# Expert weights asked for in column quarters, routing ahead of a low part, and a first token tile scaled by ScalarE in a two-layer hybrid kernel

## The chip, the cores and the metric

The kernel runs on one core of one Trainium2 chip. The metric is device microseconds from start to end of one execution. The core has TensorE (PE in the profile, with its weight loads as PEld), VectorE (DVE), ScalarE (ACT), GpSimd (POOL) and SyncE (SP), whose queue issues all DMAs of this kernel. Engines run on their own and meet at semaphores.

## What is computed

Two layers over 512 tokens of width 1024, in float32. Cut to what matters here:

```python
for l in range(2):
    h = rms_norm(x, norm_mix_g[l])
    parts = split(h @ w_in[l])            # attention, spatial gate, state space, branch gates
    y_a, y_b, y_c = attention(parts), spatial_gating(parts), s5_layer(parts)
    x = x + (g_a * y_a + g_b * y_b + g_c * y_c) @ w_mix_o[l]
    h = rms_norm(x, norm_ffn_g[l])
    # router: best of 4 groups, then the 2 best of its 8 experts, for every token
    x = x + sum over the 2 chosen experts e of weight * ((silu(h @ w_gate[e]) * (h @ w_up[e])) @ w_down[e])
out = rms_norm(x, norm_final_g)
```

There are 32 experts. The gate, up and down weights of each are 2 MB, so a layer streams 192 MB of expert weights.

## The kernel before

Tokens lie in 4 tiles of 128 (NT = 4), the width in 8 parts of 128 (ND = 8). Many products are made from a rounded high part and a low remainder (h_hi and h_lo, w_hi and w_lo, x_hi and x_lo), to keep float32 precision. Each engine has a hand-written order of work; nothing is scheduled by a planner.

**Prologue (L411 to L474).** ScalarE squares the four token tiles (`square_tokens`, L356), VectorE scales each tile (L366) and TensorE transposes it into two PSUM banks (`turn_tile`, L381). VectorE also prepares rope angles; ScalarE takes their two sines (L471, L473) at the end. All engines meet at the end of the block, and the layer's block starts.

**Start of a layer.** SyncE asks for the small tables (L520 to L523). VectorE multiplies the transposed tiles by the norm's weights, two operations of 128x512 for each tile, into `hT` (L1463). TensorE waits for the first tile (`hT_ready`) and starts `token_job` (L671). VectorE waits for `step_ready` from ScalarE (L1218, which waits for small tables), runs a long chain of small operations for the state space layer, then makes `h_lo` of the four tiles (`low_tokens`, L1532) between low parts of weights (L1545). The first `feature_job` (L649) needs `h_hi` and low weights, and for its last 8 products (x16 and x8 in the trace are one job's records) the `h_lo` of all four tiles.

**End of the dense part.** TensorE mixes (L968), transposes tiles for the router (L988), computes logits (L1000), ranks tokens within experts (L1008, L1015) and gathers the tokens of the first four experts (`gather_tile`, L1026). VectorE's order for tile 3 is `take_h2(3)`, `inverse(3)`, `low_part(3, 0, 4)` (L1843), `route(3)` (L1851 to L1867), `placed(3)` (L1874, L1875), `low_part(3, 4, 8)`, then `take` (L1922) of the gathered tokens twice, once for each half of the width. `low_part` needs `x_hi` of the tile from ScalarE (L1382); `route` needs the logits from TensorE.

**Experts.** They go in 16 pairs. For a pair, TensorE does gate and up of expert 0 and of expert 1 (`gate_up`, L1109, L1110, 6.9 us each), adds back the rows of the pair before (L1083, L1084), gathers for the next quad (L1072, L1074), transposes, and multiplies by the down weights of both (L1100). In the last two pairs nothing is gathered. Weights have two places, one for each expert of a pair. SyncE's loop asks for gate and up of expert 2i+2+b when `gu_done` reaches 2i+b+1 (L511, L512), and for both down weights of the next pair when `down_done` reaches 2i+2 (L515). The 12 MB of the first pair are asked for before the loop.

**Between the layers.** The last rows are added, squared, scaled and transposed into PSUM for the next layer. Every engine reads the largest token count of an expert and branches on it (none overflows). `clear` (L2308) is a barrier (L2312), a clearing of about 190 semaphores by SyncE, and a second barrier (L2314). The next layer's block follows.

Of the kernel before, what the change touches and what calls it, by code (L numbers as in the profile page):

```python
# [22 lines left out]
ALU = mybir.AluOpType  # L23
# [3 lines left out]
P = 128  # L27
D = 1024
S = 512
L = 2  # L30
NT = S // P
# [79 lines left out]
QUAD = 4 * CAP  # L111


def build(nc, io):
    ctx = ExitStack()
    with ctx:
# [46 lines left out]
        hT = view(O_HT, ND, S)  # L163
        slab = [O_SLAB + i * SLAB for i in range(3)]
# [213 lines left out]
        def turn_tile(t):  # L378

            for d in range(ND):  # L380
                nc.tensor.transpose(ps[:, BANK_X[t][d // 4], (d % 4) * P:(d % 4 + 1) * P], x_unit[:, t, d * P:(d + 1) * P], ident)  # L381

        def turn_tokens(pe, g):

            for t in range(NT):
                pe.wait_ge(g["xn"], t + 1)
                turn_tile(t)
# [12 lines left out]
        stack_made = so["ov_y"]  # L400

# [9 lines left out]
        with nc.Block() as block:  # L411
# [14 lines left out]
            def _(pe):  # L426
                pe.wait_ge(s["pro_in"], 32)
                turn_tokens(pe, turn_g)
# [36 lines left out]
            def _(act):  # L465
# [30 lines left out]
        shared = dict(nsa_parted="ov_silu", outp_free="ov_weights", m_hi_ready="ov_sel", m_lo_ready="ov_gathered", br_hi_ready="ov_xe", br_lo_ready="ov_gu",  # L496
# [4 lines left out]
        for layer in range(L):  # L501
# [15 lines left out]
            with nc.Block() as block:  # L517
                @block.sync
                def _(sp):
# [72 lines left out]
                    with sp.Fori(0, N_EXP // 2 - 1) as i:  # L592
# [24 lines left out]
                def _(pe):  # L617
# [34 lines left out]
                    def nsa_job(t):  # L652

                        for k in range(ND):
                            r = 32 * (k % 4)
                            last = nc.tensor.matmul(ps[r:r + 32, BANK_S[0], t * P:(t + 1) * P], wnsa[k], hT[:, k, t * P:(t + 1) * P],
# [10 lines left out]
                    def token_job(n, w, lo, hi, t):  # L667

                        out = bank_p(n)
                        for k in range(ND):  # L670
                            last = nc.tensor.matmul(out[:, 0:hi - lo], hT[:, k, t * P:(t + 1) * P], w[:, k, lo:hi],  # L671
# [14 lines left out]
                    for t in range(NT):  # L686
                        pe.wait_ge(s["hT_ready"], t + 1)
# [425 lines left out]
                    def pair(i, m, at, first, second, last_quad):  # L1113

                        q = at % 2
                        for b in range(2):
                            pe.wait_ge(w_in_sem[b][0], 16 * i + 16)
                            pe.wait_ge(w_in_sem[b][1], 16 * i + 16)
                            if b == 1 and not first:
                                pe.wait_ge(s["y_read"], 2 * i - 1)  # L1120
# [1307 lines left out]
```

## Time and profile before

| | |
|---|---|
| time, median of 3 runs | 1911.43 us (1910.63 to 1912.46) |
| the profiled execution | 1910.96 us, span 1909.2 us |
| TensorE busy | 1848.6 us, 97% |
| VectorE, ScalarE, GpSimd busy | 52%, 25%, 8% |
| HBM read | 476.59 MB, 252 GB/s over the span |

An engine's busy share alone doesn't say what bounds a stretch. The timeline says what runs when and how long an engine was idle before it; the waits name who ended the idle time; the windows give DMA rate and granted clock for a stretch; the DMA view tells how long each transfer took from issue to landing.

### The profile page before, as it was taken

How to read it: one execution, taken by the hardware profiler on the slowest of the kernel's cores; microseconds unless marked ns; L12 is line 12 of the kernel's file. 1: busy time of each engine (PE TensorE's matmuls, PEld its weight loads, DVE VectorE, ACT ScalarE, POOL GpSimd, SP SyncE). 2: the span in 40 equal slices, each digit the busy share in tenths (PEclk: the TensorE clock that was granted, in tenths of full speed). 3: DMA queues.
4: the chain of work that ended last, by engine and by line, in shares of the span. 5: the costliest groups of instructions: out<-in, count | busy, mean ns of one | idle time of the engine just before them, and what ended most of it. 6: DMA issues, size and time to landing. Idle time of an engine off the chain costs nothing. (4 is left out here: it accounts for less than half of the span.)

```text
span 1909.2 us, 26714 instructions
## 1 busy us (share of the span) xinstructions
PE 1848.6 (97%) x10376; PEld 1156.9 (61%) x10377; DVE 990.3 (52%) x1929; ACT 483.7 (25%) x858; POOL 151.2 (8%) x241
## 2 busy tenths in 40 slices
PE   6999999999999999999889999999999999999996
PEld 3777777778545445454347877778775445455442
DVE  7755556667334343343478555567673344343344
ACT  4413444432111111111234234444321110111112
POOL 4600000050000000000054000000500000000000
PEclk9999999999999999999989999999999999999998
DMA  4222111344999999999722221114359999999994
GB/s 170 67 98 85 67 67 45 111 140 190 377 428 427 419 428 427 427 428 417 314 65 77 95 68 65 67 45 133 118 226 423 427 424 425 429 427 427 423 428 175
DMA packets 59952, 482.13 MB, mean 253 GB/s; under 512 B 9808, under 2 KB 22608, under 8 KB 30672
## 3 DMA queue, kind: packets, MB, share of 16 engines
q1 hardware_dynamic: 59856, 480.80, 62.1%
q8 instruction: 66, 1.08, 0.2%
q14 instruction: 30, 0.25, 0.0%
HBM read 476.59 MB, written 4.19 MB: 252 GB/s over the span
## 5 line engine op out<-in xcount | busy, mean ns | idle before, releaser
L1932 DVE TENSOR_TENSOR x_tokens<-x_tokens,ps 128x512 f32<-128x512 f32 x240 | 160.3, 686 | 216.5 <-PE ps L1084 215.5
L1109 PE MATMUL ps<-slabs,arena 128*64 128x512 f32 x512 | 228.4, 599 | 4.3 <-issue 4.3
L1110 PE MATMUL ps<-slabs,arena 128*64 128x512 f32 x512 | 228.4, 600 | 0.0
L1100 PE MATMUL ps<-arena,branch 128*64 128x512 f32 x512 | 227.0, 596 | 0.5 <-ACT branch L1403 0.5
L1100 PE MATMUL ps<-slabs,branch 128*64 128x512 f32 x512 | 227.0, 595 | 0.0
L1109 PE MATMUL ps<-arena 128*64 128x512 f32 x512 | 225.0, 592 | 0.9 <-DVE arena L1922 0.9
L1110 PE MATMUL ps<-arena 128*64 128x512 f32 x512 | 225.0, 592 | 0.0
L822 PE MATMUL ps<-h_hi,w_parts 128*128 128x512 f32 x768 | 210.8, 408 | 1.5 <-DVE w_parts L1545 1.5
L1109 PEld LDWEIGHTS ps<-slabs,arena 128*64 128x64 f32 x512 | 70.7, 138 | 151.9 <-issue 151.9
L822 PEld LDWEIGHTS ps<-h_hi,w_parts 128*128 128x128 f32 x768 | 135.1, 189 | 38.8 <-issue 9.2
L1109 PEld LDWEIGHTS ps<-arena 128*64 128x64 f32 x512 | 70.0, 137 | 145.8 <-issue 145.8
L1100 PEld LDWEIGHTS ps<-arena,branch 128*64 128x64 f32 x512 | 67.3, 137 | 133.7 <-issue 132.7
L1938 DVE TENSOR_TENSOR branch<-ps,branch 64x512 f32<-64x512 f32 x64 | 44.1, 689 | 196.2 <-ACT branch L1399 195.3
L1399 ACT ACTIVATE branch<-ps 64x512 f32<-64x512 f32 x64 | 37.9, 592 | 399.6 <-PE ps L1110 399.6
L1977 DVE SCALAR_TENSOR_TENSOR split_rows<-ps,arena,split_rows 128x512 fp32r<-128x512 f32 x64 | 48.0, 751 | 147.1 <-ACT split_rows L1409 147.1
L1409 ACT ACTIVATE split_rows<-ps,arena 128x512 fp32r<-128x512 f32 x64 | 44.0, 687 | 308.3 <-PE ps L1100 291.7
L1545 DVE TENSOR_TENSOR w_parts<-slabs,w_parts 128x512 fp32r<-128x512 f32 x176 | 119.3, 738 | 4.5 <-ACT w_parts L1228 3.9
L1072 PE MATMUL ps<-split_rows,h_lo 128*128 128x256 f32 x448 | 115.4, 281 | 0.0
L1074 PE MATMUL ps<-split_rows,x_lo 128*128 128x256 f32 x448 | 115.1, 280 | 0.0
L822 PE MATMUL ps<-h_lo,w_parts 128*128 128x512 f32 x384 | 108.1, 406 | 0.0
L1083 PE MATMUL ps<-split_rows 128*128 128x512 f32 x240 | 103.9, 433 | 0.0
L1228 ACT ACTIVATE w_parts<-slabs 128x2048 fp32r<-128x2048 f32 x50 | 95.5, 1909 | 30.9 <-DMA slabs<-in_dense 30.9
(361 smaller groups left out, 3094.0 us busy)
## 6 DMA issues: line engine op xcount, KB each, us to landing
arena<-in_expert_w_gate SPq DMA_DIRECT2D x32, 2048.0 KB, 12.1
slabs<-in_expert_w_gate SPq DMA_DIRECT2D x32, 2048.0 KB, 15.0
slabs<-in_expert_w_up SPq DMA_DIRECT2D x32, 2048.0 KB, 19.4
arena<-in_expert_w_up SPq DMA_DIRECT2D x32, 2048.0 KB, 16.5
arena<-in_expert_w_down SPq DMA_DIRECT2D x32, 2048.0 KB, 9.5
slabs<-in_expert_w_down SPq DMA_DIRECT2D x32, 2048.0 KB, 13.9
slabs<-in_gate_w SPq DMA_DIRECT2D x24, 1024.0 KB, 4.8
slabs<-in_dense SPq DMA_DIRECT2D x22, 1024.0 KB, 5.8
```

Source lines behind the costliest of these rows:

```text
L822: last = nc.tensor.matmul(fill.out, wp[:, k % ND, (n % 2) * P:(n % 2 + 1) * P], hp[:, k % ND, :], start=(k == 0), stop=(k == GATE_MM - 1))
L1072: nc.tensor.matmul(ps[:, bank + part // 4, col:col + QUAD], x_hi[:, t, d * P:(d + 1) * P], sel[:, t, :], start=(t == 0), stop=False)
L1074: last = nc.tensor.matmul(ps[:, bank + part // 4, col:col + QUAD], x_lo[:, t, d * P:(d + 1) * P], sel[:, t, :], start=False, stop=(t == NT ...
L1083: nc.tensor.matmul(out, to, y_hi[:, cols], start=True, stop=False)
L1100: done = nc.tensor.matmul(ps[64 * b:64 * b + 64, BANK_Y[half], :], hidT[:, k, CAP * b:CAP * (b + 1)], w_down[b][:, k, half * 512:(half + 1 ...
L1109: nc.tensor.matmul(ps[0:64, BANK_GU[b], :], xk, low[:, k, :], start=(k == 0), stop=(k == ND - 1), tile_position=(0, 0))
L1110: return nc.tensor.matmul(ps[64:P, BANK_GU[b], :], xk, high[:, k, :], start=(k == 0), stop=(k == ND - 1), tile_position=(0, 64))
L1228: nc.scalar.activation(w_hi[k % 3], view(slab[k % 3], SLAB // 2), ACT.Identity).then_inc(s["w_hi_ready"], 1)
L1545: v.tensor_tensor(w_lo[k][:, part], view(slab[k], SLAB // 2)[:, part], w_hi[k][:, part], ALU.subtract)\
L1932: v.tensor_tensor(xs, xs, ps[:, banks[n % len(banks)], :], ALU.add).then_inc(s["back_added"], 1)
L1938: v.tensor_tensor(hid[rows], ps[other, BANK_GU[b], :], silu[rows], ALU.mult).then_inc(s["hid_done"], 1)
L1977: v.scalar_tensor_tensor(y_lo[:, cols], ps[:, BANK_Y[half], :], w_slot, y_hi[:, cols], ALU.mult, ALU.subtract).then_inc(s["y_lo_ready"], 1)
```

## The change

1. **Quarters (GU_PARTS = 4).** For expert 2, the third, gate and up are each asked for in four column quarters of 512 KB, after `gate_up` of expert 0 has done 2, 4, 6 and 8 of its 8 parts. The first pass of SyncE's loop is written out, and the loop starts at 1. TensorE's waits for the first weight place count the 3 more landings.
2. **Routing order.** For tile 3, `route(3)` stands ahead of `low_part(3, 0, 4)`.
3. **First gathered tokens.** Of the 4 parts in each half, VectorE takes 2 (one operation of half the size) and ScalarE the other 2, each 128x256 from PSUM with a scale (`xe_first`).
4. **First token tile.** ScalarE scales the 8 parts of tile 0 at the end of the prologue, and of layer 0 for layer 1, into a place of its own (`hT_first`, where `xsT` and `h2T` are at other times). VectorE does tiles 1 to 3 in the layer's block. TensorE's first `token_job` waits for nothing from that block but the weights. The two sines of the prologue move into ScalarE's part of layer 0.
5. **Waits and clearing.** TensorE's waits for `y_read`, each beside one for `y_lo_ready`, are gone. Between the layers the barrier ahead of the clearing is gone.

```diff
+GU_PARTS = 4
+        hT_first = view(O_XS, ND, P)
+        def tile_of(t):
+            return hT_first if t == 0 else hT[:, :, t * P:(t + 1) * P]
+        def first_tile(layer, told):
+            for d in range(ND):
+                nc.scalar.activation(hT_first[:, d, :], ps[:, BANK_X[0][d // 4], (d % 4) * P:(d % 4 + 1) * P], ACT.Identity,
+                                     scale=gmix[:, 8 * layer + d:8 * layer + d + 1]).then_inc(told, 1)
...
                 square_tokens(act, turn_g, pro_x)
-                act.wait_ge(s["pro_dve"], N_REDUCE)
-                nc.scalar.activation(rope_sin, rr, ACT.Sin).then_inc(s["pro_act"], 1)
-                act.wait_ge(s["pro_dve"], 2 + N_REDUCE)
-                nc.scalar.activation(rope_cos, r2, ACT.Sin).then_inc(s["pro_act"], 1)
-                act.wait_ge(s["pro_act"], 2)
+                act.wait_ge(s["pro_gmix"], 16 * L)
+                act.wait_ge(first_turned, 1)
+                first_tile(0, first_turned)
...
-                    with sp.Fori(0, N_EXP // 2 - 1) as i:
+                    for part in range(GU_PARTS):
+                        if part < GU_PARTS - 1:
+                            sp.wait_ge(s["gu_part"], part + 1)
+                        else:
+                            sp.wait_ge(s["gu_done"], 1)
+                        cols = slice(part * SLAB // GU_PARTS, (part + 1) * SLAB // GU_PARTS)
+                        for m, name in enumerate(("expert_w_gate", "expert_w_up")):
+                            sp.dma_start(w_place[0][m][:, cols], expert_rows(io[name], 2, ND)[:, cols]).then_inc(w_in_sem[0][m], 16)
+                    sp.wait_ge(s["gu_done"], 2)
+                    load_gate_up(sp, 3, 1)
+                    sp.wait_ge(s["down_done"], 2)
+                    for b in range(2):
+                        load_down(sp, 2 + b, b)
+                    with sp.Fori(1, N_EXP // 2 - 1) as i:
...
-                        pe.wait_ge(s["hT_ready"], t + 1)
+                        if t >= 1:
+                            pe.wait_ge(s["hT_ready"], t)
...
-                        pe.wait_ge(s["y_read"], 2 * i)
                         pe.wait_ge(s["y_lo_ready"], 2 * i)
...
+                                if first and b == 0 and k % 4 >= 2:
+                                    pe.wait_ge(s["xe_first"], 2 * (k // 4) + k % 4 - 1)
                                 done = gate_up(k, b, i, m, at)
+                                if first and b == 0 and k < ND - 1 and (k + 1) % (ND // GU_PARTS) == 0:
+                                    done.then_inc(s["gu_part"], 1)
...
+                    for half in range(2):
+                        act.wait_ge(s["x_gathered"], half + 1)
+                        for k in (4 * half + 2, 4 * half + 3):
+                            nc.scalar.activation(xe[0][:, k, :], ps[:, BANK_GATHER0 + 2 * half + 1, (k % 2) * QUAD:(k % 2 + 1) * QUAD], ACT.Identity,
+                                                 scale=small["gffn"][:, k:k + 1]).then_inc(s["xe_first"], 1)
...
+                    if not last_layer:
+                        act.wait_ge(s["next_turned"], 1)
+                        first_tile(layer + 1, s["next_turned"])
...
-                    for t in range(NT):
+                    for t in range(1, NT):
...
                     inverse(3)
+                    route(3)
                     low_part(3, 0, 4)
-                    route(3)
                     placed(3)
                     low_part(3, 4, ND)
...
-                        take(0, half, BANK_GATHER0 + 2 * half)
+                        v.tensor_tensor(xe[0][:, 4 * half:4 * half + 2, :], ps[:, BANK_GATHER0 + 2 * half, :].rearrange("p (b c) -> p b c", c=QUAD),
+                                        gf(4 * half, 2, QUAD), ALU.mult).then_inc(s["xe_ready"], 1)
...
-                clear(nc, layer_sems)
+                nc.sync.sem_clear(range(layer_sems[0].num, layer_sems[-1].num + 1))
+                nc.all_engine_barrier()
```

## Rows read from the trace of the kernel before

**Rows 1.** TensorE's waits, whole span: line, who ended them, sum, times, longest.
```profile
PE ps L1008 <- DVE arena L1867: 5.1, 4, 1.7
PE ps L1109 <- issue: 4.3, 2, 2.3
```

**Rows 2.** Timeline, prologue's end: start, duration, engine, line, then idle before.
```profile
16.13 0.20 ACT L351 ACTIVATE arena<-arena 128x1 f32<-128x1 f32 x1 [1.08 <-DVE arena L372]
...
18.41 0.63 ACT L473 ACTIVATE arena<-xn_tokens 128x512 f32<-128x512 f32 x1
...
19.52 4.87 DVE L1463 TENSOR_TENSOR hT<-ps,arena 128x512 f32<-128x512 f32 x8 [1.15 <-PEq L411]
...
20.96 13.97 PE L671 MATMUL ps<-slabs,hT 128*128 128x512 f32 x32 [2.49 <-DVE hT L1463]
```

**Rows 3.** ScalarE's durations: two of the timeline, and a page group (mean ns).
```profile
51.29 0.60 ACT L1239 ACTIVATE arena<-ps 128x512 f32<-128x512 f32 x1
51.78 0.41 ACT L1242 ACTIVATE branch<-arena 128x256 f32<-128x256 f32 x1
...
L1409 ACT ACTIVATE split_rows<-ps,arena 128x512 fp32r<-128x512 f32 x64 | 44.0, 687 | 308.3 <-PE ps L1100 291.7
```

**Rows 4.** Timeline, layer 0: the last h_lo and the products that need it.
```profile
53.55 1.22 DVE L1532 TENSOR_TENSOR h_lo<-hT,h_hi 128x1024 fp32r<-128x1024 f32 x1
...
54.91 2.02 PE L649 MATMUL ps<-h_lo,w_parts 128*128 128x512 f32 x8
```

**Rows 5.** Timeline: start of layer 1, and its last h_lo.
```profile
964.62 4.87 DVE L1463 TENSOR_TENSOR hT<-ps,arena 128x512 f32<-128x512 f32 x8 [8.51 <-PEq L2314]
...
999.28 1.23 DVE L1532 TENSOR_TENSOR h_lo<-hT,h_hi 128x1024 fp32r<-128x1024 f32 x1 [0.31 <-PE ps L656]
...
1002.81 1.98 PE L649 MATMUL ps<-h_lo,w_parts 128*128 128x512 f32 x8
```

**Rows 6.** SyncE's wait at the second barrier between the layers.
```profile
SPq L2314 <- PEq L2314: 0.5, 1, 0.5
```

**Rows 7.** Timeline, layer 0: TensorE and VectorE from tile 3's logits to expert 0.
```profile
466.01 1.87 PE L1000 MATMUL ps<-arena,branch 128*128 128x36 f32 x16
...
468.59 1.24 DVE L1843 SCALAR_TENSOR_TENSOR x_lo<-x_tokens,arena,h_lo 128x512 fp32r<-128x512 f32 x1 [2.33 <-ACT h_lo L1382]
469.74 0.25 DVE L1851 SCALAR_TENSOR_TENSOR arena<-ps,arena 128x36 f32<-128x36 f32 x1
...
473.43 0.41 PE L1008 MATMUL ps<-arena 128*128 128x32 f32 x2 [1.71 <-DVE arena L1867]
...
474.90 0.74 PE L1026 MATMUL ps<-split_rows,h_lo 128*128 128x256 f32 x4 [0.40 <-DVE split_rows L1875]
...
477.52 0.61 PE L1109 MATMUL ps<-arena 128*64 128x512 f32 x1 [0.47 <-DVE arena L1922]
```

**Rows 8.** Window 480 to 484: busy times, clock, DMA share, GB/s; expert 2's gate issue.
```profile
480.00:484.00 4.00, 4.00 (x21) 1.58 (x19) 3.73 (x9) 0.62 (x2) 0.00 (x0) 1.00 0.19 78
...
484.80 0.35 SPq L511 DMA_DIRECT2D arena<-in_expert_w_gate  x1
```

**Rows 9.** DMA view of 484 to 496, last figure us to landing: expert 2's gate.
```profile
arena<-in_expert_w_gate SPq DMA_DIRECT2D x1, 2048.0 KB, 7.8
```

**Rows 10.** DMA view, first down weight of a pair, issued at 503.4, 829.0, 888.2.
```profile
arena<-in_expert_w_down SPq DMA_DIRECT2D x1, 2048.0 KB, 9.6
...
arena<-in_expert_w_down SPq DMA_DIRECT2D x1, 2048.0 KB, 8.6
...
arena<-in_expert_w_down SPq DMA_DIRECT2D x1, 2048.0 KB, 10.1
```

**Rows 11.** Timeline, layer 0, expert 31's gate and up: the first, and a slow one.
```profile
922.82 0.61 PE L1109 MATMUL ps<-slabs,arena 128*64 128x512 f32 x1 [1.98 <-issue]
...
924.33 1.06 PE L1109 MATMUL ps<-slabs,arena 128*64 128x512 f32 x1
```

**Rows 12.** Window 6 to 8 us, loads of x and weights: last three clock, DMA share, GB/s.
```profile
6.00:8.00 2.00, 0.00 (x0) 0.00 (x0) 1.22 (x3) 0.20 (x1) 1.08 (x4) 1.00 1.03 413
```

More of the change, by code:

```diff
@@ L380, in turn_tile, with turn_tokens @@
             for d in range(ND):
-                nc.tensor.transpose(ps[:, BANK_X[t][d // 4], (d % 4) * P:(d % 4 + 1) * P], x_unit[:, t, d * P:(d + 1) * P], ident)
-        def turn_tokens(pe, g):
+                last = nc.tensor.transpose(ps[:, BANK_X[t][d // 4], (d % 4) * P:(d % 4 + 1) * P], x_unit[:, t, d * P:(d + 1) * P], ident)
+            return last
+        def first_tile(layer, told):
+            for d in range(ND):
+                nc.scalar.activation(hT_first[:, d, :], ps[:, BANK_X[0][d // 4], (d % 4) * P:(d % 4 + 1) * P], ACT.Identity,
+                                     scale=gmix[:, 8 * layer + d:8 * layer + d + 1]).then_inc(told, 1)
+        def turn_tokens(pe, g, told):
             for t in range(NT):
                 pe.wait_ge(g["xn"], t + 1)
-                turn_tile(t)
+                last = turn_tile(t)
+                if t == 0:
+                    last.then_inc(told, 1)
         s = {n: sem(n) for n in ("pro_in", "pro_gmix", "pro_table", "pro_dve", "pro_act", "pro_x0", "pro_x1", "pro_x2", "pro_x3")}
@@ L670, in token_job @@
                         for k in range(ND):
-                            last = nc.tensor.matmul(out[:, 0:hi - lo], hT[:, k, t * P:(t + 1) * P], w[:, k, lo:hi],
+                            last = nc.tensor.matmul(out[:, 0:hi - lo], tile_of(t)[:, k, :], w[:, k, lo:hi],
                                                     start=(k == 0), stop=(k == ND - 1))
@@ L1116, in pair @@
                         for b in range(2):
-                            pe.wait_ge(w_in_sem[b][0], 16 * i + 16)
-                            pe.wait_ge(w_in_sem[b][1], 16 * i + 16)
+                            more = 0 if first or b == 1 else 16 * (GU_PARTS - 1)
+                            pe.wait_ge(w_in_sem[b][0], 16 * i + 16 + more)
+                            pe.wait_ge(w_in_sem[b][1], 16 * i + 16 + more)
                             if b == 1 and not first:
-                                pe.wait_ge(s["y_read"], 2 * i - 1)
                                 pe.wait_ge(s["y_lo_ready"], 2 * i - 1)
@@ L1174, in _ @@
                     for half in range(2):
-                        pe.wait_ge(s["y_read"], N_EXP - 1 + half)
                         pe.wait_ge(s["y_lo_ready"], N_EXP - 1 + half)
@@ L1185, in _ @@
                             pe.wait_ge(s["next_xn"], t + 1)
-                            turn_tile(t)
+                            last = turn_tile(t)
+                            if t == 0:
+                                last.then_inc(s["next_turned"], 1)
                 @block.scalar
@@ L1223, in _ @@
                     nc.scalar.activation(cos1, sincos[3], ACT.Sin).then_inc(s["polar_ready"], 1)
+                    if layer == 0:
+                        nc.scalar.activation(rope_sin, rr, ACT.Sin).then_inc(s["pro_act"], 1)
+                        nc.scalar.activation(rope_cos, r2, ACT.Sin).then_inc(s["pro_act"], 1)
                     def split_hi(k):
@@ L1531, in low_tokens @@
                         cols = slice(t * P, (t + 1) * P)
[L1532 removed]
+                        v.tensor_tensor(h_lo[:, :, cols], tile_of(t), h_hi[:, :, cols], ALU.subtract).then_inc(s["h_lo_ready"], 1)
                     lows = [0]
@@ L1632, in rope @@
                         dve.wait_ge(s["rot_done"], i + 1)
+                        if layer == 0 and i == 0:
+                            dve.wait_ge(s["pro_act"], 2)
                         part = ps[:, BANK_T[i % 2], :]
@@ L2224, in _ @@
                         square_tokens(act, turn_g, None)
+                        if not last_layer:
+                            act.wait_ge(first_turned, 1)
+                            first_tile(layer + 1, first_turned)
                     @block.sync
```

15 lines of the change are left out of this document (8 added, 7 removed).

## The prediction, made before the changed kernel was seen

> **What bounds the kernel now.** I read the page first: TensorE is busy for 1848.6 of 1909.2 us, so a change can win little more than TensorE's idle time, and each piece of it has to be read where it lies. The waits say who ends it [rows 1]. Three places matter here: the start of each layer, the stretch from the router to the first expert, and the last expert of each layer. The timeline gives each its size. In layer 0 TensorE waits 2.49 us for its first product [rows 2], 1.71, 0.40 and 0.47 us on the way to expert 0 [rows 7], and 1.98 us for expert 31's weights [rows 11]; layer 1 repeats these (2 of 2 in [rows 1] for expert 31, 2.3 us there), with a longer start.
>
> The expert stretch has two limits that nearly meet. A middle pair takes TensorE 29.6 us, and the 12 MB of a pair take the DMA engines about 29.5 us. The proof is the landing time of a pair's first down weight: 9.6 us after its issue in the first pair, 8.6 in the twelfth, so DMA gains about 0.1 us a pair; then it loses 1.5 us within two pairs (10.1) [rows 10]. The last pairs are shorter for TensorE (25.8 us, nothing is gathered), and DMA, with that backlog, is 2 us late for expert 31.
>
> **Prologue and start of layer 0.** ScalarE drops two sines at the end of the prologue and gets 8 scalings of 128x128 from PSUM. No row has that shape. From 0.60 us for 512 columns and 0.41 for 256, 128 columns take about 0.31; the scale from memory adds 0.09 (0.687 against 0.60); two in a row overlap by 0.11 (the second begins 0.49 after the first) [rows 3]. So 8 x 0.29 + 0.1 = 2.4 us, from 16.33, where its last root ends, to 18.75; before, the sines ended at 19.04 [rows 2]. Bounds: with no per-column part 8 x 0.2 = 1.6, with 0.41 each and no overlap 3.3. The block then starts 0.3 us earlier (between 0.7, VectorE's own end, and -0.6). TensorE needs no VectorE operation any more: its first product moves from 20.96 to about 19.35, 0.15 us after the block's start at 19.2, 1.6 us earlier. The first weights landed by 17.1, ahead of it.
>
> Most of this is lost 35 us later. `feature_job` needs `h_lo` of tile 3, ready at 54.77, and uses it at 54.91: slack 0.1 us [rows 4]. VectorE's chain to it has no idle time above chain latency from 24.5 on, and it begins with ScalarE's `step_ready`, which waits for small tables asked for at the block's start. Taking 2 of 8 operations off VectorE ahead of that (1.2 us) therefore gives nothing; the chain moves by the block's 0.3 us only. The two sines, 1.3 us on ScalarE ahead of its first evacuation, delay that to about 30.4, and TensorE wants the bank at 34: hidden by 3 us. Gain in layer 0: 0.3 + 0.1 slack, **0.35 us** (0 to 0.8).
>
> A rule speaks against moving this: the Trainium skill ("ScalarE: Activation LUTs", Rules for kernel authors) sends plain multiplies to VectorE. The trace agrees that VectorE is quicker here, 2 x 0.6 against 2.4 us [rows 2, 3]; by the rule the move would cost 1.2 us a layer. I don't follow it, because the work falls where ScalarE has nothing else.
>
> **Between the layers.** ScalarE's 2.4 us fall into the 8.5 us in which VectorE and ScalarE stand still, while TensorE transposes the other tiles: hidden. TensorE's start behind the block's start shrinks from 1.44 us (964.62 to 966.06) to about 0.15: 1.3 us. One barrier less: the remaining one was waited for 0.5 us [rows 6]; with the clearing that now runs beside TensorE's branch I take 0.7 (0.4 to 1.2). Here nothing takes it back: the last `h_lo` is ready at 1000.51, after a wait for TensorE itself, and used at 1002.81, slack 2.3 us [rows 5]. **2.0 us** (1.5 to 2.6).
>
> **Router to expert 0, each layer.** The logits of tile 3 are out at 467.9, yet `route(3)` starts at 469.74, behind `x_hi` and `low_part` [rows 7]. Moved ahead, it starts 1.8 us earlier and ends at 471.6, where TensorE has just run out of gathers (471.7): `rank(3)` at 471.75 instead of 473.43. Now `low_part` (1.24 us) lies between `route` and `placed`, till 472.8, while the rank is there at 472.5: 0.25 us are given back, so the gather of tile 3 goes from 474.90 to 473.45, 1.45 us. Its second low half is there in time (by 474.5, used at 475.0). The first gathered half then costs VectorE one operation of half the size (0.69 us) instead of 1.24, beside TensorE's last gathers, and the 0.47 us wait goes. ScalarE's parts take 0.5 us each and are wanted 1.7 us after the first. Expert 0 starts at 475.6, not 477.52: **1.9 us** a layer (1.4 to 1.95). Its gate and up landed by 473.
>
> **Quarters, each layer.** DMA runs dry at about 481 (share 0.19 in 480 to 484) and expert 2 is asked for at 484.8 [rows 8], landing 7.8 us later [rows 9]. The first quarter's request comes at about 477.4, while the queue is still full, so the stream goes on without a gap and expert 2's weights land 5.3 us earlier. But the next request, expert 2's down weight, waits for `down_done`, which moves only with TensorE, 1.9 us. It landed 9.6 us after its issue, and a transfer into an empty queue takes 7.8 to 8.2. So the lead is cut: DMA can gain 9.6 - 8.0 = 1.6 us on TensorE, of which 0.6 to 1.0 was gained by itself later anyway (8.6) [rows 10]. After the 1.5 us that DMA loses, the landing is at 9.4 instead of 10.1: **0.7 us** (0.6 to 0.9) off the wait for expert 31. It stays, with 1.3 us in layer 0 and 1.6 in layer 1.
>
> The clock is the larger part. After the wait of 1.98 us six pairs of products ran slow, at 1.06 instead of 0.59 us, a granted 1.2 GHz; they were 1.7 us longer [rows 11]. Layer 1's wait of 2.31 was followed by the same, 1.7 us. The waits of 1.71 us ahead of `rank(3)` were not: expert 0's products run at 0.61 [rows 7]. With 1.3 and 1.6 us both new waits are below that, so I take **1.7 us** a layer (0 to 1.7).
>
> TensorE's dropped waits for `y_read` stood beside waits that imply them: 0, at most 0.05 a pair.
>
> **Sum.** 0.35 + 2.0 + 2 x (1.9 + 0.7 + 1.7) = 10.95, about 11 us. The profiled execution took 1910.96, which makes 1900.0; it was 0.5 below the median, so 1900.5 for the median.
>
> **Rivals.**
> 1. *The clock still falls* after the shorter wait, in one layer or both: 1.7 or 3.4 us less gain, 1902.2 to 1903.9. For it: only two rows tell where the line lies, and 1.6 is near 1.71.
> 2. *The wait for expert 31 goes wholly*, if DMA keeps more of its 5.3 us lead or loses less near the end: 1.3 + 1.6 us more, 1897.6. Against: the 7.8 to 8.2 us floor is seen in all first requests.
> 3. *The saved microseconds are handed on*: `placed` or ScalarE's parts come last instead and the clearing is on the path. Half of 2.0 and of 2 x 1.9 gone, and the clock too: 1904 to 1908. It covers the case that an edit doesn't do what it says.
> 4. *Slower: the quarters are slow transfers.* If eight transfers of 512 KB needed more than the 9.8 us of two whole ones by over 5.3 us, expert 2 would land later than before and, since DMA makes up only 0.1 us a pair, the whole stream would end later. The gain of 0.35 + 2.0 offsets 1.2 a layer, so the kernel is slower from 6.5 us extra a layer. At twice the time, 9.8 us extra, it would be 2 x 4.5 - 2.35, about 1918. Against: x is loaded in pieces of 512 KB with the same rows of 4 KB, beside weights, at 413 GB/s [rows 12]. The Trainium skill ("DMA: Bandwidth & Descriptors", Measured and Anatomy of one DMA) advises at least 1 MiB a transfer and gives 2.0 us fixed for each; six more transfers in a row would by that be an estimated 12 us extra a layer, and the result about 1922. The trace disagrees, since transfers in flight overlap.
>
> **How the numbers follow.** Forecast 0.5, rival 1 0.22, rival 2 0.13, rival 3 0.11, rival 4 0.04. The bounds of the terms widen each by 1 us or so; the range from 1896.5 to 1905 holds the forecast, rivals 1 and 2 and part of rival 3, leaving out some 0.15. A difference under 0.2% (3.8 us) can't be told from none. Faster 0.91: all but rival 4 and the worse half of rival 3. Same 0.06, slower 0.03.
>
> **What would show it.** The changed trace should have TensorE's first product near 19.35 and a new wait of about 1.2 us for `h_lo` in layer 0; in layer 1 no such wait; no wait of 1.7 at `rank(3)`; DMA share 1.0 without a gap around 482, and a short gap near 502 instead; a wait of 1.3 to 1.6 us ahead of expert 31, with its products at 0.59 after it. Products at 1.06 there speak for rival 1, no wait at all for rival 2, a later landing of expert 2 than 20 us after expert 0's start for rival 4. The step most likely wrong is the floor of 8 us and what follows for the clock.

## The result, and the profile after

The changed kernel takes 1895.64 us (median of 4 runs, 1893.32 to 1896.33), against 1911.16 for the kernel before beside it: a ratio of 0.9916, 95% interval 0.9903 to 0.9929, so 13.6 to 18.5 us faster. The forecast of 1900.5 was 4.9 us too high and its range began at 1896.5. A second set of runs gave 1896.19 and a ratio of 0.9931 (0.9917 to 0.9946).

The page of the changed kernel, profiled in a run of 1896.33 us (before: 1910.96 us, span 1909.2, TensorE busy 1848.6):

```profile
span 1894.6 us, 26685 instructions
PE 1843.7 (97%) x10376; PEld 1153.4 (61%) x10377; DVE 983.2 (52%) x1925; ACT 489.2 (26%) x881; POOL 151.4 (8%) x241
PEclk9999999999999999999989999999999999999998
```

Its waits of TensorE over the whole span (line, who ended them, sum, times, longest), which answer to [rows 1]:

```profile
PE ps L386 <- DVE arena L371: 16.6, 4, 11.8
PE ps L1135 <- issue: 4.2, 2, 2.7
PE ps L995 <- ACT w_parts L1262: 2.5, 1, 2.5
PE ps L697 <- PEq L2300: 1.9, 1, 1.9
PE ps L1035 <- DVE arena L1912: 1.7, 2, 0.9
...
PE ps L675 <- DVE h_lo L1575: 1.3, 1, 1.3
...
PE ps L1126 <- DMA slabs<-in_expert_w_down: 1.2, 1, 1.2
...
PE ps L697 <- issue: 0.9, 1, 0.9
```

The 1.7 us waits for the rank of tile 3 are gone (L1035 now has two of 0.9, for tile 2's rank), the predicted new wait for `h_lo` is there with 1.3 us, and expert 31 still waits twice (L1135). The stretches between the same instructions of both profiles put the 14.6 us of span as follows (us, after less before):

| stretch | change |
|---|---|
| start to the router's tables, layer 0 | -0.1 |
| from there to the request of expert 1's gate | -1.2 |
| that request to expert 0, layer 0 | -2.0 |
| expert 0 to the end of the turns | -0.9 |
| end of the turns to the next layer's block | -3.9 |
| block to VectorE's last `h_lo` of layer 1 | +0.9 |
| from there to the request of expert 1's gate | -1.2 |
| that request to expert 0, layer 1 | -2.0 |
| expert 0 to the request of the last norm's weights | -2.5 |
| from there to the last output's request | +0.9 |
| that request to the end | -2.6 |

The routing (-2.0 twice) is as forecast. Some entries are the clock's: in layer 0 slow products followed TensorE's wait of 2.43 us in the mix stage of the kernel before, and none followed the 2.53 us there in the changed one (-1.2); the same holds for expert 31 in both layers (-0.9 with a wait that is 0.7 longer, and -2.5 with one that is 0.8 shorter). In layer 1 the +0.9 and the -1.2 behind it belong together: TensorE reaches the products that need this `h_lo` 38.2 us after the block's start before and 37.9 after.

Two entries are neither forecast nor the clock's: the gap between the layers (3.9 us for a barrier costed at 0.7) and the very end (2.6 us, in which the change touches nothing). Both have one cause. Each instruction of a line has a row in the view of that line, also those of an engine's sequencer that the page leaves out. The columns are line, queue, kind, count, duration in ns (min/median/max) and start. These are the jumps of TensorE's sequencer past code that is not run (the rare path for overfull experts), in the kernel before, between the layers and at the end:

```profile
L2312 PEldq COMPARE_BRANCH  x1: 3677/3677/3677, 959.7 to 959.7; - x1
L2254 PEldq COMPARE_BRANCH  x1: 3446/3446/3446, 1905.4 to 1905.4; - x1
```

And in the changed kernel:

```profile
L2299 PEldq COMPARE_BRANCH  x1: 348/348/348, 955.4 to 955.4; - x1
L2304 PEldq COMPARE_BRANCH  x1: 348/348/348, 1893.4 to 1893.4; - x1
```

The other engines take 0.05 to 0.07 us for theirs and then stand at the barrier. SyncE's waits in the kernel before have a row for it:

```profile
SPq L2312 <- PEq L2312: 3.6, 1, 3.6
```

The DMA view of 959.5 to 964.6 in the kernel before, and of 955 to 961 in the changed one, shows pieces of 16 KB on a queue that carries instructions, two and one:

```profile
q8 instruction: 2, 0.03, 2.9%
```
```profile
q8 instruction: 1, 0.02, 1.6%
```

In all profiles here such a piece of 16 KB starts 0.9 to 1.1 us into each long jump and another behind it; with a short jump the first starts 1.1 us or more after the jump's start, when the jump is over. That the long jump waits for its piece fits this, but no run shows it by itself, and a piece takes only 0.9 to 1.6 us.

### The profile page after: what moved, and what is told of

It reads as the page before. It is cut to its first block and busy times, and to the rows that moved or that the text cites. A ratio compares the mean times of both kernels' runs of the same rounds, so it can differ in the third digit from the quotient of the medians.

```text
span 1894.6 us, 26685 instructions
## 1 busy us (share of the span) xinstructions
PE 1843.7 (97%) x10376; PEld 1153.4 (61%) x10377; DVE 983.2 (52%) x1925; ACT 489.2 (26%) x881; POOL 151.4 (8%) x241
## 3 DMA queue, kind: packets, MB, share of 16 engines
q8 instruction: 65, 1.06, 0.2%
## 5 line engine op out<-in xcount | busy, mean ns | idle before, releaser
L1135 PE MATMUL ps<-slabs,arena 128*64 128x512 f32 x512 | 225.0, 592 | 4.2 <-issue 4.2
L1135 PE MATMUL ps<-arena 128*64 128x512 f32 x512 | 225.1, 592 | 0.4 <-DMA arena<-in_expert_w_up 0.4
L1136 PE MATMUL ps<-slabs,arena 128*64 128x512 f32 x512 | 225.0, 592 | 0.0
L1135 PEld LDWEIGHTS ps<-slabs,arena 128*64 128x64 f32 x512 | 70.0, 137 | 150.2 <-issue 150.2
L849 PEld LDWEIGHTS ps<-h_hi,w_parts 128*128 128x128 f32 x768 | 135.0, 188 | 38.8 <-issue 9.2
L1135 PEld LDWEIGHTS ps<-arena 128*64 128x64 f32 x512 | 69.9, 137 | 145.7 <-issue 145.4
L1262 ACT ACTIVATE w_parts<-slabs 128x2048 fp32r<-128x2048 f32 x50 | 95.5, 1910 | 30.9 <-DMA slabs<-in_dense 30.9
## 6 DMA issues: line engine op xcount, KB each, us to landing
slabs<-in_expert_w_gate SPq DMA_DIRECT2D x32, 2048.0 KB, 14.9
```

Source lines behind the costliest of these rows:

```text
L849: last = nc.tensor.matmul(fill.out, wp[:, k % ND, (n % 2) * P:(n % 2 + 1) * P], hp[:, k % ND, :], start=(k == 0), stop=(k == GATE_MM - 1))
L1135: nc.tensor.matmul(ps[0:64, BANK_GU[b], :], xk, low[:, k, :], start=(k == 0), stop=(k == ND - 1), tile_position=(0, 0))
L1136: return nc.tensor.matmul(ps[64:P, BANK_GU[b], :], xk, high[:, k, :], start=(k == 0), stop=(k == ND - 1), tile_position=(0, 64))
L1262: nc.scalar.activation(w_hi[k % 3], view(slab[k % 3], SLAB // 2), ACT.Identity).then_inc(s["w_hi_ready"], 1)
```

## The experiments

Each kernel was profiled once and timed beside the kernel before on the same chip. Differences in us are the ratio's, taken of 1910 us.

**after_again.** The changed kernel, no edit.

> The changed kernel itself, once more. Theory A (the stream of expert weights ends the mixture stage): in both layers the first product of expert 31 waits 1.5 us, the first product on the last down weights waits about 1.2 us, and the 2.7 us wait and the late landing of 18.6 us that the first profile shows ahead of expert 31 of layer 0 are one slow stretch of transfers in that execution and do not come again. Rival (the forecast's rule, that waits of up to 1.7 us leave the clock alone and waits of 2.0 us and more don't): a fall of the clock after every wait of 2.0 us or more, and none after shorter ones. Theory B for the 2.5 us by which the span ends sooner after the last output is issued (5.6 us before, 3.0 us after): if it belongs to the program it comes again; if it is one execution's, the new profile can have either. Time 1893 to 1896.5 in each case.

1896.19 us. The wait ahead of expert 31 is 1.0 and 0.9 us, and no clock falls behind it; but it falls behind the 2.0 us wait in the mix stage of layer 0, where the first profile had waited 2.5 us without a fall. The landing of 18.6 us (the up weight of the last pair of layer 0, ahead of the 2.66 us wait) did not come again, so it is not the program's; 18.1 to 18.4 us, with waits of 2.66 to 2.68, come in three other kernels here (tile_dve, low_first, y_waits_back). The short end came again (3.0 us after the last output's request). That the stream of weights ends the stage is not borne out: the last down weights were not waited for here.

**barrier_only and barrier_back.** One barrier dropped from the kernel before, and put back into the changed one.

```
-                clear(nc, layer_sems)
+                nc.sync.sem_clear(range(layer_sems[0].num, layer_sems[-1].num + 1))
+                nc.all_engine_barrier()
```

> The kernel before with one part of the change alone: between the layers the semaphores are cleared by one clear and one barrier in place of barrier, clear, barrier. Theory A (read off the two traces: from the end of the turns to the start of the next layer's block 5.8 us before, 1.9 us after): 3.9 us faster than before, 1907.3. Rival (the term of the forecast): 0.7 us faster, 0.4 to 1.2, so 1910.5. Rival 2: the gap shrinks by 3.9 us in the trace, but the layer's first products then wait for VectorE's first tile, which has to be scaled first, and half of it is lost again: 1909.

> The changed kernel with the first of the two barriers between the layers put back. Theory A: 3.9 us slower than the changed kernel, about 1899.5, and the gap between the turns' end and the next block is 5.8 us again. Rival (the forecast's term): 0.7 us slower, about 1896.4. Under A nearly all of the difference between the forecast of 10.95 us and the measured 15.5 us is this one term.

barrier_only: 1910.23, ratio 1.0003 (0.9992 to 1.0014), no difference. The gap falls from 5.8 to 4.6 us, and the jump in it still takes 3.4. barrier_back: 1898.01, 0.9939 (0.9922 to 0.9956), 1.8 us over after_again at the median, with intervals that overlap; its gap is 2.4 us against 1.9. So the barrier is worth 0.6 to 1.1 us of the gap, as the forecast had it, and the reading "3.9 us for the barrier" is wrong. In the total it can't be told.

**whole_loads and quarters_only.** The quarters taken out of the changed kernel, and put alone into the kernel before.

```
-                    for part in range(GU_PARTS):
-                        ...
-                    with sp.Fori(1, N_EXP // 2 - 1) as i:
+                    with sp.Fori(0, N_EXP // 2 - 1) as i:
```

> The changed kernel with the third expert's gate and up weights asked for whole after its place's last product, as before; all else as changed. Theory A (the stream of expert weights ends the stage, so each layer pays what its stream starts later, 0.8 us, whatever the clock does at expert 31, since a slower product there only shortens the wait for the last down weights): 0.8 us per layer, 1.6 us slower than the changed kernel in all, about 1897.2, with waits ahead of expert 31 of 2.3 us in both layers. Rival 1 (the forecast's terms: 0.7 us of wait and 1.7 us of clock per layer): 4.8 us slower, about 1900.5. Rival 2: the transfers have slack and nothing is lost, 1895.6.

> The kernel before with the quarters alone. Theory E (a lead of the transfers is lost again within three pairs: in the changed kernel the landing time of a pair's up weight starts at 15.2 us in the second pair against 17.0 before, and is 16.4 to 17.0 by the fifth, from where it goes on as with whole loads): no difference to before, 0 +- 1 us, wait ahead of expert 31 between 1 and 2.5 us. Rival (the forecast): 0.7 us a layer off the wait and the clock behind it saved, 1.7 us a layer: 4.8 us faster.

whole_loads: 1895.01, 0.9929 (0.9913 to 0.9945), the same as after_again beside it; its waits ahead of expert 31 are 1.48 and 1.53 us, not 2.3, and no slow products follow them. quarters_only: 1908.60, 0.9994 (0.9984 to 1.0004): 1.1 us faster, -0.8 to 3.1, which leaves out the 4.8 us of the first forecast. The quarters are worth nothing that can be told here. The DMA view says where the lead goes. It shows the time from issue to landing (last figure) of the up weight of the second pair, in the kernel before, where it is issued at 510.9:

```profile
arena<-in_expert_w_up SPq DMA_DIRECT2D x1, 2048.0 KB, 16.8
```

In the changed kernel, issued at 507.7:

```profile
arena<-in_expert_w_up SPq DMA_DIRECT2D x1, 2048.0 KB, 15.2
```

The lead is there, 1.6 us in layer 0 (0.8 in layer 1, 16.1 against 16.9). The pairs after it read 15.9, 17.0, 16.8 against 16.7, 16.4, 16.8: two pairs on it is gone. It went the same way in layer 1 (16.1, 16.2, 16.7, 17.2, 18.3) and in quarters_only (14.9, 15.6, 15.9, 17.1). In all profiles this time falls by 0.1 to 0.3 us a pair over most pairs and rises again, by 0.4 to 2.6 us over one or two pairs, at places that differ; so whoever starts ahead need not end ahead. What makes the rises was not tried.

The signs against slow quarters came too: the eight pieces moved at 402 to 412 GB/s (476 to 488 us), expert 2's last piece landed 17.8 us after expert 0's start (before: 20.2), the DMA share at 480 to 484 is 1.02 instead of 0.19, and 0.80 at 500 to 504.

**no_y_waits and y_waits_back.** TensorE's waits on `y_read`, which stand beside waits that imply them, out of the kernel before and back into the changed one.

```
                         pe.wait_ge(s["selT_read"], i)
-                        pe.wait_ge(s["y_read"], 2 * i)
                         pe.wait_ge(s["y_lo_ready"], 2 * i)
...
-                                pe.wait_ge(s["y_read"], 2 * i - 1)
...
-                        pe.wait_ge(s["y_read"], N_EXP - 1 + half)
```

> The kernel before with one part of the change alone: TensorE's waits on y_read are taken out (the waits on y_lo_ready that stand beside them are kept); nothing moves but the length of TensorE's program. Theory C (where TensorE's instructions lie in its program decides it): in the kernel before two jumps of TensorE's sequencer take 3.7 and 3.5 us, with a fetch of 16 KB of instructions beside each, one between the layers and one at the very end, and every engine stands at a barrier behind them; in the changed kernel the same jumps take 0.35 us, and its program has these waits fewer. So both become short here, the stretch from the turns' end to the next layer's block falls from 5.8 to about 2.5 us and that from the last output's issue to the end from 5.6 to 3.0: 5.9 us faster than before. Rival 1 (the forecast's step: these waits cost nothing): no difference. Rival 2: the program's length matters, but by another number of instructions than these: the jumps stay long here.

> The changed kernel with TensorE's waits on y_read put back, all else as changed. Theory C (place of the instructions): both long jumps are back, 5.9 us slower than the changed kernel, about 1901. Rival 1: no difference, 1895 to 1896.5. Rival 2: the other edits have shortened the program enough, and the jumps stay short.

no_y_waits: 1901.30, 0.9959 (0.9943 to 0.9974), 5.0 to 10.9 us faster than before by an edit that the forecast costed at nothing. Both jumps are short:

```profile
L2309 PEldq COMPARE_BRANCH  x1: 347/347/347, 956.7 to 956.7; - x1
L2251 PEldq COMPARE_BRANCH  x1: 351/351/351, 1896.5 to 1896.5; - x1
```

The gap is 2.5 us and the end 3.0, 5.9 us less than before. y_waits_back: 1900.02, 0.9944 (0.9931 to 0.9957), with jumps of 3.4 and 3.5 us, about 4 us over the changed kernel (3.8 by the medians, 2.5 against after_again and 5.3 against the first set by the ratios), not 5.9. The difference lies behind the gap. Where the jump is short, the products that follow are held up instead, in the changed kernel's timeline for 0.88 us after two of them:

```profile
956.48 1.86 PE L697 MATMUL ps<-slabs,branch 128*128 128x512 f32 x2 [1.91 <-PEq L2300]
959.23 2.72 PE L697 MATMUL ps<-slabs,branch 128*128 128x512 f32 x3 [0.88 <-issue]
```

With the long jump that hold-up is missing. The gap is 1.9 us in the changed kernel and 4.7 in y_waits_back, 2.8 us apart; from the turns' end to TensorE's first product on the last `h_lo` of layer 1 it is 39.8 and 40.9 us, only 1.1 apart.

**length_back.** The same number of waits put back, but each one a repeat of a wait just passed.

```
                         pe.wait_ge(s["selT_read"], i)
                         pe.wait_ge(s["y_lo_ready"], 2 * i)
+                        pe.wait_ge(s["selT_read"], i)
...
+                                pe.wait_ge(s["y_lo_ready"], 2 * i - 1)
...
+                        pe.wait_ge(s["y_lo_ready"], N_EXP - 1 + half)
```

> The changed kernel, with a repeat of a wait that TensorE has just passed (on y_lo_ready or selT_read) in each place where the kernel before had a wait on y_read. TensorE waits for nothing that it does not wait for in the changed kernel; only its program is as long as with the y_read waits. Theory C (the place of the instructions, not the waits): both long jumps are back, 3.4 us between the layers and 3.5 us at the end, 5.9 us slower than the changed kernel, about 1901 to 1902. Rival (the waits themselves did it): the jumps stay at 0.35 us, 1895 to 1896.5.

```profile
L2302 PEldq COMPARE_BRANCH  x1: 3657/3657/3657, 955.8 to 955.8; - x1
L2307 PEldq COMPARE_BRANCH  x1: 3606/3606/3606, 1894.6 to 1894.6; - x1
```

1900.60, 0.9948 (0.9934 to 0.9962), like y_waits_back and about 4 us over the changed kernel. So it is the length of TensorE's program, or the place that this gives to later code, that makes the jumps long or short, and not anything that these waits wait for.

Both kernels have the long jumps and all the rest of the change, and that makes them a test of this rest: they are 10.7 (8.2 to 13.2) and 9.9 us (7.3 to 12.6) faster than before, where the routing alone gives 5.7 (route_only, below). From the turns' end to the request of layer 1's router tables they need 390.9 and 391.2 us, against 392.8 to 393.9 in before, before_again, quarters_only and route_only, which have long jumps too but neither the early first tile nor the dropped barrier.

**low_first and take_dve.** The two routing edits undone in the changed kernel, one each.

```
+                    low_part(3, 0, 4)
                     route(3)
-                    low_part(3, 0, 4)
                     placed(3)
```
```
-                        v.tensor_tensor(xe[0][:, 4 * half:4 * half + 2, :], ...
+                        take(0, half, BANK_GATHER0 + 2 * half)
```

> The changed kernel with the first half of tile 3's low part ahead of its routing again. The forecast's term, which theory A shares: the rank of tile 3 comes later and the gather behind it by 1.45 us, so expert 0 starts 1.45 us later in each layer: 2.9 us slower than the changed kernel. Rival (the saved time is handed on to the transfers: expert 31's weights are then waited for less): 0 to 1 us slower, with expert 0 later by 1.45 us but the wait ahead of expert 31 shorter by as much.

> The changed kernel with the first experts' gathered tokens scaled by VectorE alone again. The forecast's term: the wait of 0.47 us ahead of expert 0 comes back in each layer: 0.9 us slower than the changed kernel, 1896.6. TensorE's program is 8 waits shorter than in the changed kernel; by theory C that matters only if one of its two jumps leaves the fetched stretch, then 2.6 or 3.3 us more. Rival: ScalarE's parts take longer than VectorE's one operation, no difference.

low_first: 1902.52, 0.9955 (0.9943 to 0.9968); take_dve: 1896.53, 0.9920 (0.9906 to 0.9934). The takes bring back their wait of 0.5 us in each layer, as forecast; in the total they can't be told. The order costs more than its 2.9: 6.3 us by the medians and 4.6 by the ratios against after_again, 6.0 in the trace up to expert 0, both layers together. Its timeline in layer 1 shows the other half:

```profile
1414.29 0.41 PE L1035 MATMUL ps<-arena 128*128 128x32 f32 x2 [1.70 <-DVE arena L1912]
...
1415.77 1.23 PE L1053 MATMUL ps<-split_rows,h_lo 128*128 128x256 f32 x4
1416.79 1.06 PE L1053 MATMUL ps<-split_rows,x_lo 128*128 128x256 f32 x4
...
1419.49 1.12 PE L1135 MATMUL ps<-arena 128*64 128x512 f32 x1
```

The wait of 1.70 us is back, the same that the kernel before has [rows 7], and behind it a group of four gathers takes 1.06 us (route_only, below: 0.63). Its windows (the third number from the end is TensorE's granted clock; 0.50 is 1.2 GHz):

```profile
1412.00:1414.00 2.00, 0.60 (x6) 0.39 (x4) 1.70 (x9) 0.00 (x0) 0.00 (x0) 1.00 0.94 401
1416.00:1418.00 2.00, 2.00 (x10) 2.00 (x11) 0.92 (x2) 0.11 (x1) 0.00 (x0) 0.50 0.98 418
```

From the request of expert 1's gate to expert 0 it is 24.0 and 24.1 us, against 21.1 in the changed kernel and 23.0 in both layers of the first profile of before.

**before_again.** The kernel before, no edit.

> The kernel before, once more, for its accidents. Theory C: the two long jumps (3.7 and 3.5 us) are there again, and the route from the last gate and up request to expert 0 takes 23.0 us in both layers. The falls of the clock and the wait ahead of expert 31 may differ from the first profile (there: a fall in the mix stage of layer 0 and one behind each layer's wait for expert 31). Rival (the forecast's rule): the clock falls behind expert 31's wait of 2.0 us or more in both layers again.

1910.09 us, 0.9999 (0.9986 to 1.0011). The jumps take 3.8 and 3.8 us. The clock does not fall behind expert 31 of layer 0 (waited for 0.9 us here), and does behind the 1.70 us wait of layer 1's routing, where the first profile showed none (23.9 us to expert 0 there, not 23.0): which of the waits is followed by slow products changes from one execution to the next. Its ten runs go from 1905.04 us at a mean granted clock of 0.993 to 1914.12 at 0.988.

**route_only and lean.** The routing part alone in the kernel before; and the same with the waits on `y_read` taken out.

```
+                    route(3)
                     low_part(3, 0, 4)
-                    route(3)
                     placed(3)
...
+                    for half in range(2):
+                        act.wait_ge(s["x_gathered"], half + 1)
+                        for k in (4 * half + 2, 4 * half + 3):
+                            nc.scalar.activation(xe[0][:, k, :], ...
```

> The kernel before with the routing part of the change alone: tile 3 is routed ahead of its low part, and ScalarE scales half of the first experts' gathered tokens. Theory D (the routing pays twice: the time it saves, 1.96 us a layer in the traces, and the clock, which fell behind the 1.7 us wait ahead of the rank of tile 3, or behind its pair, in 5 of 5 kernels that have that wait in at least one layer except the first profile of before, and in none of 8 that do not have it): expert 0 starts 23.0 - 1.96 = 21.1 us after the last gate and up request in both layers, no fall of the clock within 5 us of expert 0, and the kernel is 5 to 7 us faster than before, 1904 to 1905. Rival (the forecast's terms: the saved 1.9 us a layer and nothing of the clock): 3.8 us faster, 1906.3. The long jumps are expected to stay (TensorE's program grows by 8 waits).

> The kernel before with two parts alone: the routing part as in route_only, and TensorE's waits on y_read taken out. No quarters, no dropped barrier, first tile by VectorE as before. Theory D (these two parts are nearly the whole gain): 5 to 7 us from the routing and 5 to 6 us from the jumps that become short, 11 to 13 us faster than before, 1897 to 1899, against 13 to 15.5 of the whole change. Rival (the forecast's split, in which quarters, clock behind expert 31, barrier and first tile are 7.1 of 11 us): 3.8 us faster.

route_only: 1904.05, 0.9970 (0.9958 to 0.9982), 3.4 to 8.0 us; 21.07 us from the request to expert 0 in both layers, no fall of the clock there, long jumps as before (3.7 and 3.4). Its timeline, TensorE at tile 3 of layer 0, with no wait ahead of the rank (L1008):

```profile
470.80 0.28 PE L1026 MATMUL ps<-split_rows,x_lo 128*128 128x256 f32 x1
471.05 0.41 PE L1008 MATMUL ps<-arena 128*128 128x32 f32 x2
...
472.81 0.74 PE L1026 MATMUL ps<-split_rows,h_lo 128*128 128x256 f32 x4 [0.68 <-DVE split_rows L1882]
...
474.89 0.63 PE L1109 MATMUL ps<-arena 128*64 128x512 f32 x1
```

lean: 1895.94, 0.9932 (0.9916 to 0.9947), which is the time of the whole change. An order of instructions in the routing, half of two takes, and some waits less in TensorE's program: nothing else of the change is needed where the jumps are short, though by the intervals 2 or 3 us could hide in it.

**tile_dve and down_halves.** The first tile by VectorE again, in its own place; and, as an attempt at more, the second pair's down weights in column halves, each asked for as soon as its half is free.

```
-                    for t in range(1, NT):
+                    for t in range(NT):
```
```
+                    for half in range(2):
+                        sp.wait_ge(s["down_done"], half + 1)
+                        for b in range(2):
+                            sp.dma_start(w_down[b][:, :, cols], ...)
```

> The changed kernel with the first token tile scaled by VectorE again after the block's barrier (in its own place), in both layers. The forecast's terms: TensorE's first product 1.6 us later in the prologue, of which 0.35 us reaches the end of layer 0's front, and 1.3 us later between the layers: 1.65 us slower than the changed kernel, about 1897.3. Rival (seen in the changed kernel's trace: the products that start early stand 0.9 us after the second one, and the lead has fallen by 1.1 us when the projections end): only 0.5 us in all.

> The changed kernel, and the down weights of the second pair (experts 2 and 3) are asked for in two column halves, each as soon as the first pair's products on that half are done, so the first half 3.5 us sooner. Theory A (the stream of expert weights has run dry for about 2 us at 500 to 503 us and ends the stage): 1.5 to 2 us of that gap is filled in each layer, the waits ahead of expert 31 (1.5 us) and of the last down weights (up to 1.2 us) shrink by as much, and the kernel is 2 to 4 us faster than the changed one, about 1892.5. Rival 1: 2 KB rows of the halves move slower than 4 KB rows and take back the gain: 0 to 1 us faster. Rival 2: the transfers are not what ends the stage: no difference.

tile_dve: 1897.02, 0.9928 (0.9914 to 0.9942), not told apart from the changed kernel. down_halves: 1898.02, 0.9938 (0.9926 to 0.9951), no gain either, though its down weights are asked for 3.5 us sooner; its landing time in the second pair is 14.9 us, then 17.5 in the next. It met a hold-up of 4.7 us at the start of layer 1, where the changed kernel has 0.88.

## Why the prediction was wrong, step by step

**Router to expert 0: right.** 1.9 us a layer forecast, 1.96 and 1.99 measured, 1.97 twice in route_only. The rank of tile 3 starts without a wait. What was missed is the clock: the rows showed no fall behind the 1.71 us wait, and the forecast took that as a rule. Of the profiles here, six have that wait, so twelve passes through it, and in six of the twelve slow products follow; the eleven profiles that don't have it show none there in twenty-two. At 1.7 us a fall, half of the time, that adds some 1.7 us to the 3.8, which fits the 5.7 of route_only (its interval, 3.4 to 8.0, holds 3.8 too); in low_first both layers fell, and the trace has 6.0.

**Clock behind expert 31: a step that failed.** "With 1.3 and 1.6 us both new waits are below that, so I take 1.7 us a layer". The first profile's waits in the changed kernel were 2.66 and 1.51 us and none was followed by slow products:

```profile
920.79 0.61 PE L1135 MATMUL ps<-slabs,arena 128*64 128x512 f32 x1 [2.66 <-issue]
920.79 0.64 PE L1136 MATMUL ps<-slabs,arena 128*64 128x512 f32 x1
921.24 0.59 PE L1135 MATMUL ps<-slabs,arena 128*64 128x512 f32 x1
```

In length_back a shorter wait was:

```profile
918.87 0.61 PE L1136 MATMUL ps<-slabs,arena 128*64 128x512 f32 x1 [2.00 <-issue]
...
919.75 0.94 PE L1136 MATMUL ps<-slabs,arena 128*64 128x512 f32 x1
```

Two rows can't carry a rule between them. Over the 17 profiles, waits from 1.8 us up (the mix stage's and expert 31's) were followed by a fall in 17 of 33 cases, and waits of 1.2 to 1.65 us in none of 17 (1.66 to 1.75: none of 5, against the 6 of 12 ahead of the rank). So shorter waits there did leave the clock alone, as forecast; but a longer one is followed by a fall in about half of the cases and not in all, and the forecast's 1.7 us a layer was the price of a fall taken as sure. Nor did the quarters bring it in: layer 1 of the first pair of profiles shows the forecast's 2.4 us (2.5 measured), but whole_loads, without quarters, has the same short waits and no fall. The price itself is right; the "six pairs at 1.06" behind it are five in the trace, three at 1.06 and two at 0.81 to 0.87, 1.7 us in all.

**Quarters: a step that failed.** The lead over TensorE (1.6 forecast, 1.6 measured in layer 0, 0.8 in layer 1) was right in kind; that part of it "stays" to the end was not. 0.7 us a layer was worth nothing that can be told (quarters_only: -0.8 to 3.1 us in all).

**Between the layers: terms right, sum wrong.** TensorE's start behind the block's went from 1.44 to 0.05 us (1.3 forecast), the barrier gave 0.6 to 1.1 us (0.7). "Here nothing takes it back" failed in the changed kernel: of the 1.4 us, 0.3 are left where TensorE uses layer 1's last `h_lo` (38.2 against 37.9 us after the block's start; 38.8 in after_again). A hold-up of 0.9 us behind the second product lies there, and no single-edit run shows either edit to be worth anything in the total. It holds with the long jumps: y_waits_back and length_back need 1.6 to 3.0 us less from the turns' end to layer 1's router tables than the four profiles without these two edits. With short jumps the seven profiles with the first tile by ScalarE need 388.7 to 390.5 us there, and the three with it by VectorE (no_y_waits, lean, tile_dve) 390.3 to 390.5. So the gain of these edits and that of the short jump overlap; why the hold-up comes with the short jump was not tried.

**Start of layer 0: right in kind.** ScalarE's eight scalings took 2.15 us (2.4 forecast), TensorE's first product moved from 20.96 to 19.30 (19.35), the new wait for `h_lo` is 1.3 us (1.2). About 0.1 us of it was left instead of 0.35. By the rule that the prediction weighed, plain multiplies to VectorE, the move would have cost 1.2 us a layer; tile_dve shows no difference that can be told either way (0.9928 against 0.9931).

**Dropped `y_read` waits: the step that failed most.** "0, at most 0.05 a pair". They shorten TensorE's program, and with it two jumps: 2.6 us at the end, and 3.3 between the layers (2.8 in the changed kernel); at TensorE's first product on layer 1's last `h_lo` 3.4 of these are kept in no_y_waits and 1.1 in the changed kernel. The forecast had rows that pointed there: an 8.5 us idle stretch on VectorE [rows 5], and SyncE's waits, of which it took the 0.5 us at the second barrier [rows 6] and not the 3.6 us for TensorE's queue at the first, after TensorE's last turn. It did not ask what TensorE was doing then.

**The sum.** Forecast 0.35 + 2.0 + 2 x (1.9 + 0.7 + 1.7). By the runs: routing with its clock about 5.7 (3.4 to 8.0), jumps about 5 (y_waits_back and length_back say about 4, from 2.5 to 6.1 by the ratios; no_y_waits 5.0 to 10.9), together 13 in lean (10.1 to 16.0), and 0 to 3 for all the rest. With long jumps the rest is worth more, 4 to 5 us (10.7 and 9.9 less 5.7, with some 3 us of scatter on either), and the forecast's terms for it would have looked better there than here. That the forecast came within 5 us is in part luck: 4.8 us of it, quarters and clock at expert 31, stand for gains that came from elsewhere. What stays open is the rest of no_y_waits (7.8 us) beyond the 5.9 in its trace, and how much of the 15.5 us is the runs' own scatter; the two comparisons of the same pair of kernels gave 16.0 and 13.2.

## What to carry to other kernels

An edit that removes "free" instructions still moves all code behind it. Two edits in one stretch need not add up: what one is worth depends on whether the other is in. Where engines meet at a barrier next to a jump over code that isn't run, look at the sequencers' own rows before costing the barrier, and repeat a surprising gain with the same number of harmless instructions put back. A wait of 1.7 to 3 us that is saved ahead of dense products can be worth more than its length, here by half of a fall's 1.7 us. A lead of transfers at the start of a long, nearly balanced loop is worth nothing until it is seen to last to the end.

## What the hardware did that was not expected

- A jump of TensorE's sequencer takes 0.35 us or 3.4 to 3.8 us in the same place, according to 16 waits more or less in each layer's code (50 of the some 21,600 instructions that TensorE executes, by the trace). Long ones stand in before, before_again, barrier_only, route_only, quarters_only, y_waits_back and length_back; short ones in all others.
- Where the jump is short, a hold-up of 0.5 to 4.7 us comes ahead of the first product of layer 1 or one or two products later, in seven of ten profiles (not in no_y_waits, lean and whole_loads).
- The clock's falls come and go between executions of one kernel, at 1.7 us each where TensorE is busy (twice that in two of six cases ahead of expert 0); most of the scatter of the kernel before (1905.0 to 1914.1 us in one set of ten) goes along with its mean granted clock.
- The backlog of the weight stream falls by 0.1 to 0.3 us a pair and rises again, by 0.4 to 2.6 us, at pairs that differ from execution to execution.
